# A gated residual block on one core: the gate products of two merging groups move from VectorE to GpSimd

## The reference

```
h = rms_norm(x, norm_pre);  proj = h @ w_in
u_s, z_s, q, k, v, z_r, gl_s, gl_r = split(proj)
y_s = s5_mixer(u_s, ...) * silu(z_s)          # (1024, 1024)
y_r = retention(q, k, v) * silu(z_r)          # (1024, 1024)
m   = sigmoid(gl_s) * (y_s @ w_proj_s5) + sigmoid(gl_r) * (y_r @ w_proj_ret)
x   = x + rms_norm(m @ w_out, norm_post)
```

## Time and profile before

| | us |
|---|---|
| median of 3 runs (2351.91 to 2355.09) | 2353.94 |
| the profiled execution | 2354.2 |
| its span | 2352.4 |
| TensorE busy | 2238.0 (95%) |
| VectorE busy | 1807.4 (77%) |
| ScalarE busy | 1176.1 (50%) |
| GpSimd busy | 122.2 (5%) |

### The profile page before, as it was taken

The page is one execution under the profiler, slowest core; times in us unless marked ns, Lnnn a source line. Parts: engine busy times, 40 slices in busy tenths (PEclk is TensorE's granted clock), DMA queues, the critical chain, the costliest instruction groups (busy, mean ns, idle before and its releaser), DMA issues.

```text
span 2352.4 us, 28535 instructions
## 1 busy us (share of the span) xinstructions
PE 2238.0 (95%) x10276; PEld 1836.8 (78%) x10276; DVE 1807.4 (77%) x2896; ACT 1176.1 (50%) x1958; POOL 122.2 (5%) x200
## 2 busy tenths in 40 slices
PE   6889999999999999999989999999999999999993
PEld 3678788888888888888867778887877777788883
DVE  5986992987888888655896956766787897877676
ACT  4434443456575455565435545754545544455552
POOL 5240000000000000000000100200000000000000
PEclk9999996999999999999999999999999999999997
DMA  7347555776677365579655788576745664643546
GB/s 255 143 161 233 144 183 187 255 248 210 210 249 252 105 217 184 196 259 332 223 172 155 274 254 265 164 238 220 246 152 193 219 211 148 242 163 129 169 132 265
DMA packets 265855, 485.60 MB, mean 206 GB/s; under 512 B 51648, under 2 KB 59856, under 8 KB 263536
## 3 DMA queue, kind: packets, MB, share of 16 engines
q1 hardware_dynamic: 218336, 398.54, 51.3%
q10 hardware_dynamic: 37712, 50.47, 6.1%
q0 software_dynamic: 9664, 34.75, 4.6%
HBM read 367.28 MB, written 116.39 MB: 206 GB/s over the span
## 4 chain that ended last, share of the span: by engine, by line
PE 75%; DVE 14%; issue 4%; DMA 3%; ACT 2%; ACTq 0%; DVEq 0%; SPq 0%; POOL 0%; POOLq 0%
PE psum L1745 18%; PE psum L1747 18%; PE psum L1746 18%; PE psum L1741 5%; PE psum L1742 5%; PE psum L1743 5%; DVE a_lo L1258 3%; DVE b_lo L1260 3%; DMA araw<-aops 1%; DVE work L1111 1%; DVE keep L1268 1%; PE psum L1762 1%; DVE work L1223 1%; PE psum L1681 1%; ACT work L986 1%
## 5 line engine op out<-in xcount | busy, mean ns | idle before, releaser
L1745 PE MATMUL psum<-a_hi,b_hi 128*128 128x512 f32 x2352 | 926.4, 394 | 46.0 <-DVE b_lo L1260 45.6
L1746 PE MATMUL psum<-a_hi,b_lo 128*128 128x512 f32 x2352 | 918.8, 391 | 0.0
L1747 PE MATMUL psum<-a_lo,b_hi 128*128 128x512 f32 x2352 | 918.7, 391 | 0.0
L857 ACT ACTIVATE a_hi<-araw 128x512 fp32r<-128x512 f32 x644 | 405.8, 630 | 895.5 <-PE psum L1747 656.1
L1258 DVE TENSOR_TENSOR a_lo<-araw,a_hi 128x512 fp32r<-128x512 f32 x644 | 444.3, 690 | 370.5 <-ACT a_hi L857 369.2
L1745 PEld LDWEIGHTS psum<-a_hi,b_hi 128*128 128x128 f32 x2352 | 443.6, 189 | 158.8 <-DVE b_lo L1260 61.7
L1747 PEld LDWEIGHTS psum<-a_lo,b_hi 128*128 128x128 f32 x2352 | 443.5, 189 | 93.1
L1746 PEld LDWEIGHTS psum<-a_hi,b_lo 128*128 128x128 f32 x2352 | 443.8, 189 | 91.4 <-issue 0.7
L1260 DVE TENSOR_TENSOR b_lo<-bx,b_hi 128x512 fp32r<-128x512 f32 x432 | 296.4, 686 | 0.0
L1741 PE MATMUL psum<-b_hi,a_hi 128*128 128x512 f32 x672 | 263.1, 392 | 5.1 <-DVE b_lo L1260 4.7
L867 ACT ACTIVATE b_hi<-bx 128x512 fp32r<-128x512 f32 x432 | 266.5, 617 | 0.1
(11 more groups left out here) (161 smaller groups left out, 1683.2 us busy)
## 6 DMA issues: line engine op xcount, KB each, us to landing
araw<-aops SPq DMA_DIRECT2D x632, 256.0 KB, 3.0
bz<-in_wstream SPq DMA_DIRECT2D x216, 256.0 KB, 4.4
aops<-work SPq DMA_DIRECT2D x28, 1024.0 KB, 6.8
spill<-keep ACTq DMA_DIRECT2D x28, 1024.0 KB, 5.9
bx<-in_wstream SPq DMA_DIRECT2D x108, 256.0 KB, 4.4
by<-in_wstream SPq DMA_DIRECT2D x108, 256.0 KB, 5.5
work<-spill SPq DMA_DIRECT2D x20, 1024.0 KB, 7.6
aops<-work POOLq DMA_DIRECT2D x15, 1024.0 KB, 9.1
```

Of the source, the lines that this page charges most:

```text
L857: A.activation(a_hi[:, r, :], left(s), ACT.Copy).then_inc(head, 1)
L1745: T.matmul(bank, b_hi[:, r, cols], a_hi[:, r, :], start=first, stop=False, skip_group_check=on)
L1746: T.matmul(bank, b_lo[:, r, cols], a_hi[:, r, :], start=False, stop=False, skip_group_check=on)
L1747: done = T.matmul(bank, b_hi[:, r, cols], a_lo[:, r, :], start=False, stop=last, skip_group_check=on)
```

## The change

In GWR0 and GWR1, except for the last quarter (GWR1, 6), GpSimd multiplies the gates by the kept product, in place in `gate`, once the gates have landed and the quarter is evacuated. It counts in a new semaphore `weighted`. VectorE only adds the product to m, seven steps behind the end of the block product instead of five, and waits for `weighted` first. SyncE reaches every gate load eleven steps behind instead of ten. Two semaphores are joined in one (`cleared`) to make room.

```diff
+        def by_pool(g, p):
+            return g in (GWR0, GWR1) and (g, p) != (GWR1, 6)
...
-                over = ended(s - 10)
+                over = ended(s - 11)
                 if over and GWS0 <= over[0] <= GWR1 and over[1] >= 3:
                     n = 4 * (over[0] - GWS0) + over[1] - 3 + 2
                     if n < 16:
                         load_gate(n)
...
             pool.wait_ge(yr_ops_stored, 4 * 16)
+            for g in (GWR0, GWR1):
+                for p in range(3, 7):
+                    n = 4 * (g - GWS0) + p - 3
+                    b = KEEP[p]
+                    if (g, p) == (GWR1, 6):
+                        continue
+                    pool.wait_ge(gate_loaded[n % 2], 16 * (n // 2 + 1))
+                    if p == 6:
+                        pool.wait_ge(act_evac, 4 * g + 4)
+                    else:
+                        pool.wait_ge(dve_evac, 3 * g + p - 2)
+                    gates = gate[:, n % 2, :].rearrange("p (k m) -> p k m", k=4)
+                    pool.tensor_tensor(gates, gates, kept_4(b), ALU.mult).then_inc(weighted, 1)
...
+                gates = gate[:, n % 2, :].rearrange("p (k m) -> p k m", k=4)
+                if by_pool(g, p):
+                    dve.wait_ge(weighted, n - 7)
+                    dve.wait_ge(gated, n)
+                    V.tensor_tensor(m, m, gates, ALU.add).then_inc(gated, 1)
+                    return
...
+                over = ended(s - 7)
+                if over and over[1] >= 3 and by_pool(*over):
+                    merge(*over)
                 over = ended(s - 5)
-                if over and GWS0 <= over[0] <= GWR1 and over[1] >= 3:
+                if over and GWS0 <= over[0] <= GWR1 and over[1] >= 3 and not by_pool(*over):
                     merge(*over)
...
-                        V.memset(ret_state[:, :, :], 0.0).then_inc(state_cleared, 1)
+                        V.memset(ret_state[:, :, :], 0.0).then_inc(cleared, 1)
...
-                pe.wait_ge(state_cleared, 1)
+                pe.wait_ge(cleared, 2)
```

More of the change, by code:

```diff
@@ L253, in build_program @@
         m2_full, m2_copied, m2_stored = sem("m2_full"), sem("m2_copied"), [sem(f"m2_stored{n}") for n in range(4)]
-        lags_full, lags_ready, zeros_ready, m1_stored = sem("lags_full"), sem("lags_ready"), sem("zeros_ready"), sem("m1_stored")
+        lags_full, lags_ready, cleared, m1_stored = sem("lags_full"), sem("lags_ready"), sem("cleared"), sem("m1_stored")
         m3_ready, m3_stored = sem("m3_ready"), [sem(f"m3_stored{n}") for n in range(2)]
@@ L281, in build_program @@
         gate_loaded = [sem(f"gate_loaded{n}") for n in range(2)]
-        gated, state_cleared = sem("gated"), sem("state_cleared")
+        gated, weighted = sem("gated"), sem("weighted")
         gain_row_loaded = sem("gain_row_loaded")
@@ L760, in _ @@
                 pool.dma_start(dst.rearrange("p g h -> p (g h)"), src).then_inc(params_loaded, 16)
-            pool.wait_ge(zeros_ready, 1)
+            pool.wait_ge(cleared, 1)
             for t in range(STEP - 1):
@@ L1158, in inputs_scaled @@
                 else:
-                    V.memset(zeros, 0.0).then_inc(zeros_ready, 1)
+                    V.memset(zeros, 0.0).then_inc(cleared, 1)
             def window_part(n):
@@ L1491, in merge @@
                     dve.wait_ge(dve_evac, 3 * g + p - 2)
-                gates = gate[:, n % 2, :].rearrange("p (k m) -> p k m", k=4)
                 if g < GWR0:
```

## The result

The changed kernel takes 2378.66 us (median of 4 runs, 2373.13 to 2381.86) against 2353.34 us before (4 runs): ratio 1.0111, interval 1.0095 to 1.0127, or +25 us. The forecast was 2369 us with a range up to 2376 us: the direction and most of the mechanism are right, the size is not. The profiled execution has a span of 2378.1 us, 25.7 us more than before.

A forecast was written before the change was run, and what follows sets the result against it. TensorE was taken as the bound, waiting on VectorE. Blocked time (+13.9 us) and the new order (14 to 16 us) were taken as +15 us: 2354.2 + 15 = 2369 us, range 2355 to 2376 us.

The forecast's parts named there:

- What bounds the kernel: Whole kernel: TensorE is the bound and waits on VectorE; time lost around 1900 to 2012 us reaches the end unchanged.
- The block per product: GWR0 and GWR1: each GpSimd product keeps VectorE's operations with two SBUF inputs out for 4.3 us.
- The sum at full clock: GWR0 and GWR1: blocked time less saved products gives +13.9 us, the new order 14 to 16 us; +15 us taken.
- 8.7 us piles: VectorE in both groups: evacuation, addition and blocked time together, 2.20 + 2.21 + 4.3 us without a split, against 3 us of slack.
- waits of 4 to 5 us: TensorE on `b_lo`, two or three places in each group: fewer but longer waits, some 24 us instead of 6.7 us.
- The step of GWR1 that was put at 0.9 us: A GWR1 step that does not wait before the change was to wait 0.9 us, part of the some 24 us.
- Additions two steps later and gate loads: VectorE's later additions to m: only part of the 0.9 us in GWR1; SP's gate loads one step later: costed at nothing.
- A: Rival for the two groups: GpSimd's product does not hold VectorE up; -7 us, 2347 us, chance 0.10.
- B: Rival for the two groups: GpSimd does not get in while VectorE runs back to back; +11 us, 2365 us, chance 0.13.
- Rival C: TensorE in the two groups: waits become long enough for its clock to fall; +5 us, 2374 us, chance 0.12.
- the gap of 3.15 us: Clock rival's evidence: once in the trace, ahead of a phase of small matmuls, with the granted clock going to 0.50.
- catches up meanwhile: Clock rival's +5 us: VectorE catching up partly hides half-clock steps, each 2.72 us longer, behind three or four waits.

The follow-up runs named there:

- four_pieces: Changed kernel with each GpSimd product in four instructions of 512 columns; 2365.67 us, ratio 1.0053 against the kernel before.
- filled_waits: Changed kernel with 12 matmuls of zeros on TensorE ahead of its wait at four steps; 2368.10 us, ratio 1.0065 against the kernel before.
- memset: Changed kernel with GpSimd writing zeros to the gates instead of multiplying, the seven products left out; 2344.61 us, ratio 0.9968 against the kernel before.
- one_input: Changed kernel with GpSimd copying the kept quarter to the gates instead of multiplying; 2352.83 us, ratio 0.9999 against the kernel before.
- add_at_8: Changed kernel with the additions of p = 3, 4 and 5 eight steps behind, gate loads twelve; 2366.94 us, ratio 1.0058 against the kernel before.

## Why the prediction was wrong

*What bounds the kernel* held: behind the stretch every kernel takes 305.5 to 306.9 us to the end, so what is won or lost in it arrives there.

*The block per product* held. 4.3 us was forecast from operations of 64 to 256 elements, 4.4 us was measured. The rule of the Trainium skill (SBUF — State Buffer, section "Who interferes with whom"), one holder for a whole instruction, agrees with the single operation of 5.08 us beside a long product. It says that whichever starts first holds the port; what a waiting instruction gets, the second product of four_pieces shows: a waiting GpSimd instruction was passed by eight of VectorE's.

*The sum at full clock* held: +15 forecast; the stretch without its half-clock time is +15.9 us in the changed kernel and +16.0 us in filled_waits. So did the shape, 8.7 us piles and waits of 4 to 5 us "at two or three places in each group": 4.51 and 3.70 us in GWR0, 4.51 and 3.87 us in GWR1, and 2.33 us early in GWR1, behind the fourth product. The waits were longer but not fewer, eight against six in the row. The step of GWR1 that was put at 0.9 us waited 0.85 us.

*Additions two steps later and gate loads* held: nothing is lost by them in memset.

*Rivals A and B* fell for the changed kernel: VectorE's lengthened operations exclude A, and VectorE never idled for `weighted`. A's price was nearly right, as memset shows. B's behaviour came once, in four_pieces.

*Rival C* is the step that failed: the forecast's sum has no term for the clock, and the rival that has one puts it at +5 us with a chance of 0.12. It had to be part of the forecast instead. The forecast itself had waits of 4 to 5 us, and I discounted C because these stand between dense matmuls while the gap of 3.15 us stood ahead of a phase of small ones. But that was not the only fall of the clock in the trace of the kernel before. Earlier in it, TensorE went to half clock at four waits for `b_lo` between dense matmuls, of 2.22, 3.19, 2.82 and 1.80 us, and lost 1.4 to 1.6 us at each. One of them, and its window:

```profile
1205.57 0.50 PE L1745 MATMUL psum<-a_hi,b_hi 128*128 128x512 f32 x1 [3.19 <-DVE b_lo L1260]
```

```profile
1200.00:1210.00 10.00, 6.81 (x23) 0.83 0.48 159
```

The prediction has none of these rows. The price of +5 us rested on VectorE that "catches up meanwhile". The granted clock fell at all four long waits, about one step at half clock each as C has it, and the price was 9.5 us; filled_waits won back 7.8 us for 7.9 us of it. The catching up is real but short: in the rows above the ring of three heads stops VectorE after two further steps (the idle 3.30 us), so what the slow step is late is lost. The forecast with C at this price would have been 2354.2 + 15 + 9.5 = 2379 us; that this meets 2378.66 us is closer than its terms are known.

## What to carry to other kernels

Work moved from VectorE to GpSimd was free here only where GpSimd did not read (memset); a two-operand product of 2048 columns held VectorE up for 4.4 us to save it 2.3 us. Compare each pile of work on the feeding engine with its slack ahead of TensorE, not its total with the stretch: the same work in smaller portions a step apart gained 5 us in the stretch (7 us in the whole run). Where a forecast has TensorE waiting between dense matmuls, look for half-clock time behind such waits in the trace at hand, over its whole length and not only in the stretch of the change, and add it to the sum: here each fall cost 1.4 to 2.8 us, at its full price where a short ring keeps the other engines from working ahead. No length of wait that is safe can be read from these runs.

## What was not expected of the hardware

- The granted clock fell with shorter waits than I had thought: in one_input, whose longest wait is 1.85 us, it fell at both of the waits of that length, and in add_at_8 at two of 2.35 us. It did not always fall: the changed kernel's wait of 2.33 us has full clock behind it, and of two waits in the kernel before, 1.80 us (at 1372.08) and 1.81 us (at 1999.40), only the first has half clock. What tells these apart was not settled.
- Matmuls of zeros in the wait kept the clock at 1.00 where it had been 0.70 (four times 12 of them). At a wait of 2.42 us that was not filled, one window of the same kernel shows 0.83.
- GpSimd's reading costs VectorE 2.15 ns per element with two operands and 0.83 ns with one (4.40 and 1.70 us for 2048 elements); writing alone (memset) lengthened none of its operations.
- A GpSimd instruction that is ready does not always get its turn at VectorE's next boundary. It did in 1992.16 to 2000.36 us and did not from 1902.23 us on, through eight of VectorE's instructions, in one execution of four_pieces.
